# Delta rule's triangular inverse: U made by transposing T, last level on 64x64 blocks

## The chip, the cores and the metric

One core of one Trainium2 chip runs the whole program. The metric is the device time of one execution in microseconds (us), the median of the runs. The engines are PE (TensorE's matmuls), PEld (its weight loads), DVE (VectorE), ACT (ScalarE), POOL (GpSimd) and SP (SyncE, which issues DMAs). Each engine runs its own program in order; semaphores tie them together.

## The reference

A two-layer decoder trunk: layer 0 has an RG-LRU mixer and a dense SwiGLU, layer 1 a gated delta rule (DeltaNet) and a mixture of experts; both have cross-attention. 512 prompt tokens and 8 samples of 4 tokens share the weights. What matters here is the delta rule of layer 1, for 8 heads:

```python
decay = exp(where(lower_incl, gc[..., :, None] - gc[..., None, :], -inf))
A = where(strict_lower, einsum('nbhid,nbhjd->nbhij', kb, k) * decay, 0.0)
Tinv = triangular_solve(A + eye, eye, left_side=True, lower=True, unit_diagonal=True)
u = Tinv @ vb
w = Tinv @ (kb * exp(gc)[..., None])
```

The reference takes chunks of 64 tokens; the kernel takes four chunks of 128 for the prompt, which is the same function, and one small block of 32 for the samples.

## The kernel before

**The inverse.** For each head and each of the four chunks, the inverse of the unit lower triangular 128x128 matrix is built in doubling levels. Level 0 inverts blocks of 2 rows by a subtraction; levels v = 1 to 6 join two blocks of 2^v rows into one of twice the size. The kernel keeps the inverse so far twice: `G_t` (T) and its transpose `G_u` (U), since a matmul wants its left operand transposed. `G_dt` holds the decayed Gram matrix, `G_masks` for each level the blocks that are to be joined. A level goes like this (four chunks at once; `ps` is PSUM, its second index the bank):

- PE, L984: the Gram matrix times T into bank 4. The samples' block, only at level 1, L986.
- DVE, L2131: bank 4 times the level's mask into `G_pt`.
- PE, L1001, not at level 6: U's product with `G_pt` into bank 5; DVE, L2137: T = T - bank 5.
- PE, L1005: the same product the other way round into bank 6; DVE, L2144: U = U - bank 6. At level 1 the samples' U too (L1007, L2143).

After level 6, `G_u` gives the weights and values of the recurrence (L1015, L1025 and on).

**What runs between.** The inverse is a chain, so other work is laid into it by hand, as the order of each engine's program. On PE, `fill(n)` runs n portions of six matmuls (L554) of the input projection of the head after next, two portions after most products, and in places the norms' sums (`lengths`), the transposes of the next head's keys and values (`turn_kv`, L908, L909) and its Gram products (`gram`). Heads 6 and 7 have no head after next, hence no projection left. On DVE, the work on the next two heads follows L2144 of a level: level 1 `argument` (L2004), level 3 `unit` and two taps of `convolve` (L1904, L1909), level 4 `scaled`, `damped` and `out_norm`, level 5 two more taps; `history` comes at level 2 ahead of L2137. POOL splits the arriving weights into two parts (L472, L476) as PE frees their buffers.

**Semaphores.** `d_pt`: bank 4 is full; `d_pte`: `G_pt` is written; `d_ut`: bank 5 is full; `d_tt`: T is written; `d_uu`: bank 6 is full; `d_ute`: U is written. PE waits for `d_tt` ahead of L984 and for `d_pte` and `d_ute` ahead of L1001. `s(...)` on DVE issues an operation and waits until it is done.

Of the kernel before, what the change touches and what calls it, by code (L numbers as in the profile page):

```python
# [5 lines left out]
P = 128  # L6
D, KT = 1024, 8
TP, NB, TS = 512, 8, 4
NS = NB * TS
# [9 lines left out]
GH, C, NC = 8, 128, 4  # L19
NT = NC + 1  # L20
NE, FF, FT = 8, 1536, 12
HALVES = 2
KV1_AT = {0: (0, 4), 1: (4, 8), 2: (8, 12), 3: (12, 16)}
LEVELS = 7
# [87 lines left out]
def ge(eng, sem, val):  # L112

    if isinstance(val, int) and val <= 0:
        return
    eng.wait_ge(sem, val)


def trunk(nc, I, O):
    F, R = mybir.dt.float32, mybir.dt.float32r  # L120
    ALU, ACT, AX = mybir.AluOpType, mybir.ActivationFunctionType, mybir.AxisListType
    MUL, ADD, SUB = ALU.mult, ALU.add, ALU.subtract
    ds = bass.ds

    with ExitStack() as ctx:
# [25 lines left out]
        ps = ctx.enter_context(nc.psum_tensor("ps", [P, 8, 512], F))  # L151
# [388 lines left out]
        def _(pe):  # L540
# [422 lines left out]
            def head(h):  # L963
# [14 lines left out]
                for v in range(1, LEVELS):  # L978
                    small = v < SLEVELS
                    pe.wait_ge(d_tt, h * (LEVELS - 1) + v)  # L980
                    if v == 1:
                        ge(pe, d_s, h * NC)
                    for c in range(NC):
                        last = mm(ps[:, 4, c * P:(c + 1) * P], G_dt[p][:, c, :], G_t[:, c, :], start=True, stop=True)  # L984
                    if small:
                        last = mm(ps[0:NS, 7, 352:352 + NS], G_sdt[0:NS, p, :], G_st[0:NS, :], start=True, stop=True)  # L986
                    last.then_inc(d_pt, 1)
                    fill((2, 2, 2, 2, 3, 3)[v - 1])
                    if v == 1 and h:
                        out_length(h - 1)  # L990
                    if v == 2 and h + 1 < GH:
                        lengths(h + 1, 0)
                    if v == 4 and h + 1 < GH:
                        turn_kv(h + 1)
                    if v == 5 and h + 1 < GH:
                        gram(h + 1)
                    pe.wait_ge(d_pte, h * (LEVELS - 1) + v)
                    pe.wait_ge(d_ute, h * LEVELS + v)
                    if v < LEVELS - 1:
                        for c in range(NC):  # L1000
                            last = mm(ps[:, 5, c * P:(c + 1) * P], G_u[p][:, c, :], G_pt[:, c, :], start=True, stop=True)  # L1001
                        last.then_inc(d_ut, 1)
                    ge(pe, d_vne, h * NC)
                    for c in range(NC):
                        last = mm(ps[:, 6, c * P:(c + 1) * P], G_pt[:, c, :], G_u[p][:, c, :], start=True, stop=True)  # L1005
                    if small:
                        last = mm(ps[0:NS, 7, 384:384 + NS], G_spt[0:NS, :], G_su[0:NS, p, :], start=True, stop=True)  # L1007
                    last.then_inc(d_uu, 1)
                    fill((2, 1, 3, 0, 2, 0)[v - 1])
                    if v == 2 and h + 1 < GH:  # L1010
                        lengths(h + 1, 1)
# [731 lines left out]
        def _(dve):  # L1743
# [373 lines left out]
            def head(h):  # L2117
# [8 lines left out]
                for v in range(1, LEVELS):  # L2126
                    small = v < SLEVELS
                    dve.wait_ge(d_pt, h * LEVELS + v + 1)
                    if small:
                        s(V.tensor_tensor(G_spt[0:NS, :], ps[0:NS, 7, 352:352 + NS], G_masks[0:NS, v - 1, 0:NS], MUL))  # L2130
                    s(V.tensor_tensor(G_pt, b4(4), G_masks[:, v - 1, :].unsqueeze(1).to_broadcast((P, NC, P)), MUL),  # L2131
                      d_pte, h * (LEVELS - 1) + v)
                    if v == 2 and pro:
                        history(h + 2)
                    if v < LEVELS - 1:
# [5 lines left out]
                    dve.wait_ge(d_uu, h * (LEVELS - 1) + v)  # L2141
                    if small:
                        s(V.tensor_tensor(G_su[0:NS, p, :], G_su[0:NS, p, :], ps[0:NS, 7, 384:384 + NS], SUB))  # L2143
                    s(V.tensor_tensor(G_u[p], G_u[p], b4(6), SUB), d_ute, h * LEVELS + (v + 1))  # L2144
                    if v == 1:
                        dve.wait_ge(d_egr, h + 1)
                        s(V.tensor_tensor(G_qg, G_eg[:, p, :], G_qkv[p][:, 0, :], MUL), d_qg, h + 1)
# [292 lines left out]
```

## Time and profile before

| | |
|---|---|
| median of 3 runs | 2546.24 us |
| lowest and highest run | 2544.56 and 2550.89 us |
| span of the profiled execution (its own time, first to last instruction) | 2548.9 us |
| mean granted TensorE clock, share of full speed | 0.958 |
| the eight heads of the delta rule | about 1026 to 1512 us of the span |
| PE busy over the span | 2310.6 us (91%) |
| DVE busy over the span | 905.0 us (36%) |

The profiled execution has no time of its own beside its span; the time around the span is not listed. Busy shares are means over stages with different limits. In a timeline row the first number is the start in us from the span's start, the second the length; `x8` means eight instructions in a row; the bracket is the idle time before and what ended it. A product of four chunks in fp32 shows as eight instructions.

### The profile page before, as it was taken

The page shows a single profiled execution, that of the slowest core. Times are in us where ns is not written, and L with a number is a line of the kernel's source. Part 1 is how long each engine was busy: PE and PEld are TensorE (multiplying, and loading weights), DVE is VectorE, ACT ScalarE, POOL GpSimd, SP SyncE. Part 2 cuts the span into 40 slices and gives each one's busy share as a digit, 9 for nine tenths or more (in the row PEclk, how much of TensorE's full clock was granted, in tenths as well). Part 3 has the DMA queues.
Part 4 walks back from the last instruction along what each step waited for, and adds up shares of the span by engine and source line. Part 5 has one row for each costly group of instructions (what it writes and reads, how often), then busy time and mean ns, then how long its engine had stood idle before and what let it go on. Part 6 is the DMA issues. An engine that isn't in the chain of part 4 may idle for free.

```text
span 2548.9 us, 42792 instructions
## 1 busy us (share of the span) xinstructions
PE 2310.6 (91%) x17174; PEld 2190.4 (86%) x17174; DVE 905.0 (36%) x1485; ACT 541.8 (21%) x1022; POOL 988.9 (39%) x1397
## 2 busy tenths in 40 slices
PE   8998889899999997999999788878599999999993
PEld 8988867899999987888888678848599999999993
DVE  3674423411011158777777545224101000000004
ACT  2351321310011033333333221232100000111103
POOL 4647535588888947333333007705200000000001
PEclk9999999899999999999999889999699999999996
DMA  7314442222222222122122112440456577788884
GB/s 290 99 59 160 157 158 91 91 84 89 92 83 86 87 91 69 52 62 62 62 62 62 37 44 98 182 182 17 178 182 204 193 249 242 241 257 281 280 288 159
DMA packets 98649, 348.08 MB, mean 137 GB/s; under 512 B 13504, under 2 KB 18752, under 8 KB 93616
## 3 DMA queue, kind: packets, MB, share of 16 engines
q1 hardware_dynamic: 73136, 279.08, 32.6%
q10 hardware_dynamic: 19328, 45.18, 5.2%
q0 software_dynamic: 6016, 21.43, 2.3%
q8 instruction: 122, 2.00, 0.3%
q14 instruction: 47, 0.39, 0.1%
HBM read 319.19 MB, written 26.47 MB: 136 GB/s over the span
## 4 chain that ended last, share of the span: by engine, by line
PE 63%; issue 14%; DVE 9%; POOL 6%; DMA 4%; ACT 3%; ACTq 0%; POOLq 0%; DVEq 0%; SPq 0%
PE ps L554 26%; PE ps L1144 14%; PE ps L1159 8%; PE ps L794 4%; POOL wl L476 3%; DMA raw<-weights 3%; POOL wh L472 2%; PE ps L655 1%; DVE x L1770 1%; PE ps L1005 1%; PE ps L1001 1%; PE ps L984 1%; PE ps L659 1%; PE ps L841 1%; DVE x L1758 1%
## 5 line engine op out<-in xcount | busy, mean ns | idle before, releaser
L472 POOL TENSOR_TENSOR wh<-raw,tab 128x256 fp32r<-128x256 f32 x672 | 439.7, 685 | 806.3 <-PE ps L554 541.2
L476 POOL TENSOR_TENSOR wl<-raw,wh 128x256 fp32r<-128x256 f32 x672 | 521.1, 806 | 0.0
L1144 PE MATMUL ps<-work,raw 128*128 128x128 f32 (+6 forms) x3072 | 424.3, 299 | 13.0 <-DMA raw<-weights 10.6
L1144 PEld LDWEIGHTS ps<-work,raw 128*128 128x128 f32 x3072 | 419.6, 191 | 16.3 <-issue 9.4
L554 PE MATMUL ps<-xh,wh 128*128 128x272 f32 x2048 | 306.1, 300 | 49.0 <-POOL wl L476 17.0
L554 PEld LDWEIGHTS ps<-xh,wh 128*128 128x128 f32 x2048 | 276.7, 195 | 63.6 <-issue 26.1
L554 PE MATMUL ps<-xh,wl 128*128 128x272 f32 x2048 | 297.5, 295 | 0.0
L554 PE MATMUL ps<-xl,wh 128*128 128x272 f32 x2048 | 280.9, 289 | 0.0
L554 PEld LDWEIGHTS ps<-xh,wl 128*128 128x128 f32 x2048 | 275.8, 194 | 1.8 <-issue 0.5
L554 PEld LDWEIGHTS ps<-xl,wh 128*128 128x128 f32 x2048 | 266.1, 189 | 0.0
L523 POOL DMA_DIRECT2D rows_y<-moe_h x8 | 4.3, 540 | 656.9 <-DVE moe_h L2255 656.9
L1159 PE MATMUL ps<-work,raw 128*128 128x128 f32 (+6 forms) x1536 | 218.0, 298 | 1.6 <-DVE work L2262 0.8
L1159 PEld LDWEIGHTS ps<-work,raw 128*128 128x128 f32 x1536 | 209.6, 190 | 2.4 <-DVE work L2262 1.4
L2262 DVE TENSOR_TENSOR work<-moe_h,ps 128x128 f32<-128x128 f32 (+6 forms) x96 | 30.6, 319 | 438.4 <-ACT moe_h L1678 438.4
L1678 ACT ACTIVATE moe_h<-ps 128x128 f32<-128x128 f32 (+6 forms) x96 | 29.1, 303 | 396.7 <-PE ps L1144 396.7
L1854 DVE TENSOR_TENSOR work<-work,ps 128x544 f32<-128x544 f32 x24 | 17.3, 721 | 228.6 <-PE ps L554 228.6
L2255 DVE COPY moe_h<-ps 128x256 f32<-128x256 f32 (+1 forms) x64 | 25.0, 391 | 198.0 <-PE ps L1132 155.5
L794 PE MATMUL ps<-hh,wh 128*128 128x272 f32 x384 | 79.7, 289 | 0.9 <-POOL wl L476 0.9
L794 PE MATMUL ps<-hh,wl 128*128 128x272 f32 x384 | 79.0, 288 | 0.0
L794 PE MATMUL ps<-hl,wh 128*128 128x272 f32 x384 | 78.9, 287 | 0.0
L1246 ACT ACTIVATE lnr<-x 128x544 f32<-128x544 f32 x35 | 23.1, 660 | 216.0 <-DVE x L1806 159.0
L1806 DVE SCALAR_TENSOR_TENSOR x<-x,ps 128x544 f32<-128x544 f32 x32 | 23.1, 721 | 124.3 <-PE ps L554 119.1
(378 smaller groups left out, 2987.3 us busy)
## 6 DMA issues: line engine op xcount, KB each, us to landing
raw<-weights SPq DMA_DIRECT2D x488, 512.0 KB, 4.1
moe_h<-cache SPq DMA_DIRECT2D x6, 2048.0 KB, 9.2
moe_h<-cache ACTq DMA_DIRECT2D x4, 2048.0 KB, 15.3
work<-cache SPq DMA_DIRECT2D x4, 2048.0 KB, 8.7
moe_h<-rows_x POOLq DMA_DIRECT2D x14, 512.0 KB, 8.0
rows_x<-lnsq ACTq DMA_DIRECT2D x9, 512.0 KB, 10.9
work<-scratch ACTq DMA_DIRECT2D x16, 272.0 KB, 4.2
work<-cache ACTq DMA_DIRECT2D x2, 2048.0 KB, 10.5
```

The source lines that it names most:

```text
L472: nc.gpsimd.tensor_tensor(flat(h1[:, k0:k1]), flat(r1[:, k0:k1]), one_col, MUL).then_inc(pool_hi, 1)
L476: low = nc.gpsimd.tensor_tensor(flat(l1[:, k0:k1]), flat(r1[:, k0:k1]), flat(h1[:, k0:k1]).bitcast(F), SUB)
L554: last = mm(ps[:, 2 * i + h, 0:HT], w[:, par_, k, :], a[:, k, h * HT:(h + 1) * HT], start=(n == 0 and k == 0), stop=(n == 2 and k == KT - 1))
L655: last = mm(ps[:, b, 0:MEM], raw[:, q, k, :], A_mem[:, k, :], start=(k == 0), stop=(k == KT - 1))
L659: last = mm(ps[:, b, mt * P:(mt + 1) * P], A_mem[:, k, mt * P:(mt + 1) * P], raw[:, q, k, :], start=(k == 0), stop=(k == KT - 1))
L794: last = mm(ps[:, 2 * d + h, 0:HT], w[:, s % 2, k, :], a[:, f, h * HT:(h + 1) * HT], start=(f == 0 and m == 0), stop=(f == FT - 1 and m == 2))
L841: last = mm(ps[:, 4 + 2 * (g % 2) + h, 0:HT], L_gw[:, 4 * k + g, :], L_rec[:, b % 2, k, h * HT:(h + 1) * HT], start=(k == 0), stop=(k == 1))
L984: last = mm(ps[:, 4, c * P:(c + 1) * P], G_dt[p][:, c, :], G_t[:, c, :], start=True, stop=True)
L1144: last = mm(ps[:, j // 2, (j % 2) * c:(j % 2 + 1) * c], raw[:, slot % RAW, k, :], M_x[:, r % 2, k, 0:c], start=(k == 0), stop=(k == KT - 1))
L1159: last = mm(ps[:, 2 + d % 2, 0:c], raw[:, slot % RAW, k, :], M_h[:, f, 0:c], start=(f == 0), stop=(f == FT - 1))
L1678: s(A(M_s[:, f % 2, 0:c], ps[:, f % 2, 0:c], ACT.Silu), m_silu, e12 + f + 1)
L2262: s(V.tensor_tensor(M_h[:, f, 0:c], M_s[:, f % 2, 0:c], ps[:, f % 2, c:2 * c], MUL), m_h, e12 + f + 1)
```

## The change

At levels 1 to 5, U is no longer computed by a product and a subtraction. When the new T is there, PE transposes it into bank 6 at the start of the next level, ahead of that level's product into bank 4, and DVE copies bank 6 into U. The samples' block at level 1 stays as it was, without a signal of its own. At level 6 only the lower left quarter of the product is computed (64x64x64), the mask becomes a copy of that quarter, the last product is 64x64x64 as well, and U's upper right quarter is written as its negative. The wait for bank 6 (`d_vne`) moves to the first transposes.

```diff
--- before.py
+++ after.py
@@ -19,6 +19,7 @@
 GH, C, NC = 8, 128, 4
 NT = NC + 1
 NE, FF, FT = 8, 1536, 12
+HP = P // 2
 HALVES = 2
 KV1_AT = {0: (0, 4), 1: (4, 8), 2: (8, 12), 3: (12, 16)}
 LEVELS = 7
@@ -980,8 +981,17 @@
                     pe.wait_ge(d_tt, h * (LEVELS - 1) + v)
                     if v == 1:
                         ge(pe, d_s, h * NC)
+                    else:
+                        if v == 2:
+                            ge(pe, d_vne, h * NC)
+                        for c in range(NC):
+                            last = nc.tensor.transpose(ps[:, 6, c * P:(c + 1) * P], G_t[:, c, :], ident)
+                        last.then_inc(d_uu, 1)
                     for c in range(NC):
-                        last = mm(ps[:, 4, c * P:(c + 1) * P], G_dt[p][:, c, :], G_t[:, c, :], start=True, stop=True)
+                        if v < LEVELS - 1:
+                            last = mm(ps[:, 4, c * P:(c + 1) * P], G_dt[p][:, c, :], G_t[:, c, :], start=True, stop=True)
+                        else:
+                            last = mm(ps[HP:P, 4, c * P:c * P + HP], G_dt[p][0:HP, c, HP:P], G_t[0:HP, c, 0:HP], start=True, stop=True)
                     if small:
                         last = mm(ps[0:NS, 7, 352:352 + NS], G_sdt[0:NS, p, :], G_st[0:NS, :], start=True, stop=True)
                     last.then_inc(d_pt, 1)
@@ -1000,12 +1010,13 @@
                         for c in range(NC):
                             last = mm(ps[:, 5, c * P:(c + 1) * P], G_u[p][:, c, :], G_pt[:, c, :], start=True, stop=True)
                         last.then_inc(d_ut, 1)
-                    ge(pe, d_vne, h * NC)
-                    for c in range(NC):
-                        last = mm(ps[:, 6, c * P:(c + 1) * P], G_pt[:, c, :], G_u[p][:, c, :], start=True, stop=True)
-                    if small:
-                        last = mm(ps[0:NS, 7, 384:384 + NS], G_spt[0:NS, :], G_su[0:NS, p, :], start=True, stop=True)
-                    last.then_inc(d_uu, 1)
+                        if small:
+                            mm(ps[0:NS, 7, 384:384 + NS], G_spt[0:NS, :], G_su[0:NS, p, :], start=True, stop=True)
+                    else:
+                        for c in range(NC):
+                            last = mm(ps[0:HP, 6, c * P + HP:(c + 1) * P], G_pt[HP:P, c, 0:HP], G_u[p][HP:P, c, HP:P],
+                                      start=True, stop=True)
+                        last.then_inc(d_uu, 1)
                     fill((2, 1, 3, 0, 2, 0)[v - 1])
                     if v == 2 and h + 1 < GH:
                         lengths(h + 1, 1)
@@ -2128,8 +2139,11 @@
                     dve.wait_ge(d_pt, h * LEVELS + v + 1)
                     if small:
                         s(V.tensor_tensor(G_spt[0:NS, :], ps[0:NS, 7, 352:352 + NS], G_masks[0:NS, v - 1, 0:NS], MUL))
-                    s(V.tensor_tensor(G_pt, b4(4), G_masks[:, v - 1, :].unsqueeze(1).to_broadcast((P, NC, P)), MUL),
-                      d_pte, h * (LEVELS - 1) + v)
+                    if v < LEVELS - 1:
+                        s(V.tensor_tensor(G_pt, b4(4), G_masks[:, v - 1, :].unsqueeze(1).to_broadcast((P, NC, P)), MUL),
+                          d_pte, h * (LEVELS - 1) + v)
+                    else:
+                        s(V.tensor_copy(G_pt[HP:P, :, 0:HP], b4(4)[HP:P, :, 0:HP]), d_pte, h * (LEVELS - 1) + v)
                     if v == 2 and pro:
                         history(h + 2)
                     if v < LEVELS - 1:
@@ -2141,7 +2155,11 @@
                     dve.wait_ge(d_uu, h * (LEVELS - 1) + v)
                     if small:
                         s(V.tensor_tensor(G_su[0:NS, p, :], G_su[0:NS, p, :], ps[0:NS, 7, 384:384 + NS], SUB))
-                    s(V.tensor_tensor(G_u[p], G_u[p], b4(6), SUB), d_ute, h * LEVELS + (v + 1))
+                    if v < LEVELS - 1:
+                        s(V.tensor_copy(G_u[p], b4(6)), d_ute, h * LEVELS + (v + 1))
+                    else:
+                        s(V.tensor_scalar(G_u[p][0:HP, :, HP:P], b4(6)[0:HP, :, HP:P], -1.0, None, MUL),
+                          d_ute, h * LEVELS + (v + 1))
                     if v == 1:
                         dve.wait_ge(d_egr, h + 1)
                         s(V.tensor_tensor(G_qg, G_eg[:, p, :], G_qkv[p][:, 0, :], MUL), d_qg, h + 1)
```

## Rows read from the trace of the kernel before

**Rows 1.** Windows, heads 4 and 6: us, then busy us (instructions) of PE, PEld, DVE, ACT, POOL; PEclk; DMA.

```profile
1281.30:1344.60 63.30, 59.68 (x483) 55.35 (x483) 46.30 (x82) 21.14 (x42) 21.95 (x33) 1.00 0.21 62
...
1407.90:1466.10 58.20, 44.17 (x289) 37.48 (x289) 33.13 (x60) 15.46 (x29) 4.58 (x6) 0.85 0.09 30
```

**Rows 2.** Groups by line, DVE, the eight heads: busy, mean ns, idle before, releasers.

```profile
L2131 DVE TENSOR_TENSOR work<-ps,moe_h 128x512 f32<-128x512 f32 x48 | 33.2, 691 | 16.8 <-PE ps L984 15.3 <-DVE work L2005 0.2
...
L2137 DVE TENSOR_TENSOR moe_h<-moe_h,ps 128x512 f32<-128x512 f32 x40 | 27.5, 688 | 60.0 <-PE ps L1001 59.7
```

**Rows 3.** Timeline of head 4, levels 1 to 3: start, length, engine, line.

```profile
1288.31 0.69 DVE L2144 TENSOR_TENSOR work<-work,ps 128x512 f32<-128x512 f32 x1
...
1289.41 0.98 PEld L984 LDWEIGHTS ps<-moe_h,work 128*128 128x128 f32 x8
...
1291.62 0.69 DVE L2131 TENSOR_TENSOR work<-ps,moe_h 128x512 f32<-128x512 f32 x1
...
1292.61 1.09 PEld L1001 LDWEIGHTS ps<-work 128*128 128x128 f32 x8
...
1294.00 0.69 DVE L2137 TENSOR_TENSOR moe_h<-moe_h,ps 128x512 f32<-128x512 f32 x1
...
1296.07 1.09 PEld L984 LDWEIGHTS ps<-moe_h,work 128*128 128x128 f32 x8
...
1298.58 0.99 PEld L1001 LDWEIGHTS ps<-work 128*128 128x128 f32 x8
```

**Rows 4.** Timeline of head 4, levels 3 to 5.

```profile
1300.76 0.69 DVE L2144 TENSOR_TENSOR work<-work,ps 128x512 f32<-128x512 f32 x1 [0.20 <-PE ps L1005]
...
1302.63 0.98 PEld L984 LDWEIGHTS ps<-moe_h,work 128*128 128x128 f32 x8
...
1304.40 0.69 DVE L2131 TENSOR_TENSOR work<-ps,moe_h 128x512 f32<-128x512 f32 x1
...
1306.13 0.97 PEld L1001 LDWEIGHTS ps<-work 128*128 128x128 f32 x8
...
1308.30 0.69 DVE L2144 TENSOR_TENSOR work<-work,ps 128x512 f32<-128x512 f32 x1 [0.20 <-PE ps L1005]
...
1314.84 0.69 DVE L2131 TENSOR_TENSOR work<-ps,moe_h 128x512 f32<-128x512 f32 x1
...
1315.58 0.97 PEld L1001 LDWEIGHTS ps<-work 128*128 128x128 f32 x8 [0.75 <-DVE work L2131]
```

**Rows 5.** Timeline of head 4, levels 5 and 6.

```profile
1317.74 0.69 DVE L2144 TENSOR_TENSOR work<-work,ps 128x512 f32<-128x512 f32 x1 [0.20 <-PE ps L1005]
...
1318.86 0.98 PEld L984 LDWEIGHTS ps<-moe_h,work 128*128 128x128 f32 x8
...
1320.64 0.69 DVE L2131 TENSOR_TENSOR work<-ps,moe_h 128x512 f32<-128x512 f32 x1
...
1322.00 0.98 PEld L1005 LDWEIGHTS ps<-work 128*128 128x128 f32 x8
...
1323.28 0.69 DVE L2144 TENSOR_TENSOR work<-work,ps 128x512 f32<-128x512 f32 x1 [1.07 <-PE ps L1005]
```

**Rows 6.** Timeline: transposes of the next head's keys.

```profile
1305.04 0.48 PEld L908 LDWEIGHTS ps<-tab,x 128*128 128x128 f32 x4
...
1305.48 0.10 PEld L909 LDWEIGHTS ps<-tab,x 128*32 128x32 f32 x1
```

**Rows 7.** Single DVE lines, whole kernel: ns min/median/max, first and last start.

```profile
L2174 DVE COPY work<-ps x8: 292/293/293, 1077.0 to 1503.2; 128x128 f32<-128x128 f32 x8
...
L2004 DVE SCALAR_TENSOR_TENSOR work<-work,tab x32: 351/352/695, 999.0 to 1419.2; 128x128 f32<-128x128 f32 x32
...
L1909 DVE SCALAR_TENSOR_TENSOR work<-work,par x64: 810/812/1172, 55.6 to 1405.0; 128x568 f32<-128x568 f32 x64
```

**Rows 8.** Timeline, POOL: first part of the weight splitting.

```profile
1292.17 2.33 POOL L472 TENSOR_TENSOR wh<-raw,tab 128x256 fp32r<-128x256 f32 x4 [6.21 <-PE ps L554]
...
1305.40 2.33 POOL L472 TENSOR_TENSOR wh<-raw,tab 128x256 fp32r<-128x256 f32 x4 [8.15 <-PE ps L554]
```

## What the change does to the time: the prediction

> **What bounds the kernel now.** I read the page first (span 2548.9 us; TensorE busy nearly throughout), then the stretch of the delta rule alone, because all edits lie in its eight heads. The windows table gives one line a head. Head 4 takes 63.3 us, with PE busy 59.7 and DVE 46.3 at a granted clock of 1.00; head 6, which has no projection work left to fill with, takes 58.2 us at 0.85 [rows 1]. Heads 0 to 5 repeat head 4's pattern (head 0 is a little shorter). A busy share of 94% looks as if PE set the time. The groups by line and the timeline say something else: the two engines hand data to and fro inside each level, each in its own program order. Over the eight heads DVE waited 59.7 us before the subtraction from T (L2137) for the product L1001, and 15.3 us before the mask (L2131) for L984 [rows 2]. So I follow one head through its levels and ask at each hand-over which side comes last.
>
> Names, for level v: P is the product into bank 4 (L984), M the mask (L2131), Q the product into bank 5 (L1001), S the subtraction giving the new T (L2137), R the old product into bank 6 (L1005), U the update of U (L2144), F the projection matmuls that PE runs between them. In head 4 DVE runs S and U back to back and then its other work for the next heads (history, argument, unit, convolve, scaled, damped, out_norm), while PE runs R, then F, then the next P. At levels 2, 3 and 4 Q starts straight after PE's own preceding work: P3 to Q3 takes 2.51 us [rows 3]. At level 5 it starts 0.74 us after M, that is as M ends [rows 4]. Both sides are nearly balanced, and DVE's side work is hidden under F.
>
> **The change, part by part.** *R at levels 1 to 5 goes.* Eight matmul instructions per R (an fp32 product shows as two). Q3 to P4 is 4.05 us for Q, R and eighteen F matmuls [rows 3, 4]; of an eight-instruction product PE's issue is 0.88 us (eight at 0.11, the spacing below). *Four transposes come in its place*, after the wait for the new T and ahead of the next P. The transposes of the key rows, of the same kind and 128x128 size, show as one instruction each: four start 0.44 us before the next group, so 0.11 us each [rows 6]. PE therefore issues 0.44 us less per level. A result reaches DVE 1.28 us after an eight-instruction product starts (L1005 at 1322.00, U at 1323.28 [rows 5]); with four fewer, 1.28 - 0.44 = 0.84 us after the first transpose.
>
> But the place matters more than the work. Before, U's operand was computed before F; now DVE's copy into U waits until PE has run F, has seen the new T and has transposed it. Behind that copy on DVE stand all the side jobs of the level, then M; PE's next Q waits for M. U's copy itself costs what the subtraction did (a copy lies on the same line of sizes, below), so nothing is gained there.
>
> Head 4, with a dash for the time after the change. I move P back by the 0.88 us of the missing R wherever PE's own work sets it.
> - Level 1 to 2: P2 was at 1289.41, so the transposes start at 1288.53; U', behind the sample rows' small subtraction (0.21 with its gap), at 1288.53 + 0.84 + 0.21 = 1289.58, 1.27 later than 1288.31. M2' follows at 1291.62 + 1.27 = 1292.89, Q2' 0.75 later (M's 0.69 and 0.06) at 1293.64 instead of 1292.61: **+1.03** [rows 3]. PE, ready at 1288.97 + 3.20 = 1292.17, waits about 1.5 us.
> - Level 2 to 3: transposes at Q2' + (3.46 - 0.88) = 1296.22 (S, at 1294.00 + 1.27 and 0.69 long, is done), P3' 1296.66, Q3' 2.51 later, 1299.17: +0.59 in all, so **0.44 given back** [rows 3].
> - Level 3 to 4: transposes at 1299.17 + 4.05 - 0.88 = 1302.34, U' at 1303.18, 2.42 later than 1300.76. Two normalisations and two convolution taps follow; M4' 3.64 after U' at 1306.82, Q4' 1307.57 against 1306.13: **+1.44 in all** [rows 4].
> - Level 4 to 5: no F here, so S ends last: 1.28 + 0.69 + 0.05 = 2.02 after Q4', then 0.84: U' at 1310.43 against 1308.30. M5' 6.54 later, Q5' at 1317.71 against 1315.58: **+2.13 in all** [rows 4].
> - Level 5 to 6: transposes at Q5' + (3.28 - 0.88) = 1320.11, U' 1320.95, M6' 2.90 later at 1323.85 [rows 5].
> - *Level 6, 64x64.* M becomes a copy of 4x64 columns. A 128-column copy takes 0.29 [rows 7], a 512-column operation 0.69 [rows 2]; a straight line gives 0.42 for 256. The last R starts at 1323.85 + 0.42 + 0.06 = 1324.33. No 64-column product is in the trace: at 128 columns' price DVE goes on 1.28 later, at half the issue 0.84; I take 0.84, since the 0.11 spacing is that of 128 moving columns. U's last step, again 256 columns, 0.42: done at 1325.59. Before: 1323.28 + 0.69 = 1323.97 [rows 5]. **Head 4: +1.6 us**; with both 64x64 savings nil, 0.27 + 0.44 + 0.27 more, +2.6. The smaller P of level 6 saves nothing: F and U's side work cover it.
>
> *A collision.* POOL's splitting starts when F ends a weight tile: 1292.17 and 1305.40, some 2.76 us after P2 and P4 [rows 8]. P moves earlier than, or with, its old place and DVE's side work moves later, so the last of the four 128x128 operations of the argument and the convolution tap now run under POOL. Those operations take 352 ns alone and up to 695, the tap 812 and up to 1172 [rows 7]. Nil to 0.69 (two of the four) and nil to 0.36: I take one of each, 0.34 + 0.36 = **0.7 a head**.
>
> Heads 0 to 5: 6 x (1.6 + 0.7) = 13.8 us. Heads 6 and 7 have no F: each of five levels puts 0.44 between S and P, up to 2.2; where M follows P at once, this is on the path (that wait is the 15.3 us of [rows 2]). Level 6 gives back 0.98. That is +1.2 at most; nil if the lengths and side work still end later. I take 0.7 each. Sum: 13.8 + 1.4 = **+15 us**. Nothing after the heads has slack against them: the output projection reads their result. The profiled span, 2548.9, is 2.7 above the runs' median; added to the median, 2546.2 + 15 = 2561.
>
> The Trainium skill's "TensorEngine Tiling (Array Packing)", sections Overview and Tiling Modes, says that a 64x64 product uses one of four independent tiles, at best four times the rate. No row here shows 64x64; all four chunks use the same tile in this diff, so I don't count on it. By that rule the last R's issue would be an estimated 0.22 instead of 0.44, the sum 8 x 0.22 = 1.8 us less.
>
> **The rivals.**
> 1. *PE's own work is the bound after all* (faster). Place: heads 0 to 5, PE busy 94%. If no M ends after F, only PE's savings count: 5 x 0.44 + 0.44 = 2.6 us a head, 8 heads, 21 us: 2525. For it: Q2 to Q4 start behind PE's own work. Against: those have less than a microsecond of slack, while U moves 1.3 to 3.2 us. It decides only if DVE's copy into U can come within about 0.3 us of the old place. Chance 0.07.
> 2. *The delays are swallowed* (same): F that no longer fits moves to the head's end, where PE waits often, and the 64x64 steps are cheaper than taken. Six heads at nil to 1 us: 2546 to 2553. Chance 0.13.
> 3. *The clock falls.* With more idle time and fewer matmuls, heads 0 to 5 could behave as head 6, granted 0.85 [rows 1]. A mean of 0.85 is 0.30 of the stretch at 1.2 GHz, at most 0.15 x 63 = 9.5 us of PE time a head; with a quarter on the path, 2.4 x 6 = 14 us more: 2575. Against: head 4 already has waits of 0.5 to 1 us without a fall. The Trainium skill's "Perfetto Trace Analysis", Matmul Optimizations, speaks for this rival: power scales with utilisation, so matmuls should run back to back; head 6's row agrees. Chance 0.10.
> 4. *The forecast*: 2554 to 2573. Lower end: no collision, 6 x 1.6 = 9.6, less up to 2 for cheaper small steps. Upper end: both collisions whole (1.05) and the 64x64 savings nil (2.6): 6 x 3.65 + 4 = 26. Chance 0.70.
>
> **How the numbers follow.** The bound for no change is 0.3%, 7.6 us, so 2538.6 to 2553.9. Faster 0.07 (rival 1), same 0.13 (rival 2), slower 0.80 (forecast and rival 3). The range reaches from the middle of rival 2, 2550, to the low edge of rival 3, 2574; what lies outside is rival 1, half of 2 and part of 3.
>
> **What would show it.** Right: in a head with F, U's copy waits for the transposes, 2 us and more at levels 3 and 5; Q2, Q4 and Q5 wait for M; the heads 0 to 5 become about 2.3 us longer, 6 and 7 by less than 1.5; transposes at 0.11 us spacing; the argument or the tap lengthened under POOL. Wrong: heads shorter than 63.3 us, Q still directly behind F at levels 3 to 5, or PEclk under 1.00 in heads 0 to 5, which would put the cost elsewhere.

## The result and the profile after

The changed kernel takes 2585.04 us (median of 4 runs, 2581.29 to 2590.43) beside 2548.56 us for the kernel before (4 runs on the same chip, 2544.56 to 2551.18): ratio 1.0137, 95% interval 1.0115 to 1.0159. It is slower, as forecast, but by 36 us and not by 15, and the time lies outside the range.

The two profiled spans differ by 30.6 us (2548.9 and 2579.5). Up to head 0's first subtraction (before L2123, now L2134) the profiles differ by -1.5 us; the eight heads, from there to the last copy of outputs, go from 482.0 to 513.5 us, **+31.5**; the rest of the program differs by +0.6. So in these two profiles the whole loss lies in the heads, where the edits are. The profiled execution of the changed kernel is the fastest of its four; the others took longer at lower mean granted clocks (spans of 2579.5, 2581.5, 2584.9 and 2588.6 us at 0.947, 0.945, 0.943 and 0.937), so the medians differ by more than the two profiles.

The windows of the kernel after: heads 3, 4 and 6, then head 7 up to U's last step, and from there to the outputs. Columns as in [rows 1].

```profile
1228.50:1294.20 65.70, 57.84 (x463) 52.11 (x462) 47.01 (x82) 21.09 (x42) 22.70 (x33) 1.00 0.21 60
1294.20:1361.67 67.47, 60.77 (x463) 55.00 (x462) 47.02 (x81) 21.09 (x42) 22.70 (x33) 0.95 0.19 58
...
1427.36:1488.32 60.96, 43.44 (x269) 36.00 (x269) 32.65 (x60) 15.50 (x29) 4.59 (x6) 0.80 0.09 29
1488.32:1520.40 32.08, 20.52 (x124) 17.14 (x124) 17.34 (x27) 5.37 (x6) 0.00 (x0) 0.83 0.10 33
1520.40:1545.00 24.60, 21.09 (x105) 17.64 (x106) 6.76 (x12) 4.49 (x10) 0.00 (x0) 0.50 0.01 3
```

The same stretch from U's last step of head 7, in the kernel before:

```profile
1496.87:1515.00 18.13, 13.82 (x104) 11.15 (x105) 7.05 (x12) 4.50 (x10) 0.00 (x0) 0.88 0.02 5
```

Two kinds of loss are to be seen. Head 3 ran at full clock throughout (1.00, as head 4 before in [rows 1]) with PE doing 1.8 us *less* than there, and still took 65.70 instead of 63.3 us. Heads 1 and 5 agree (65.76, 65.69). Head 4 did the same instructions in 67.47 us at a granted clock of 0.95, and everything after U's last step in head 7 ran at 0.50, which is 1.2 of 2.4 GHz. A stretch granted 0.50 is called a half-rate stretch below.

DVE's groups in the eight heads show what the copy into U waits for. U's old subtraction (L2144) had waited 15.2 us for PE in all.

```profile
L2159 DVE COPY work<-ps 128x512 f32<-128x512 f32 x40 | 27.7, 692 | 41.7 <-PE ps L988 41.3 <-DVE work L2157 0.2
L2143 DVE TENSOR_TENSOR work<-ps,moe_h 128x512 f32<-128x512 f32 x40 | 27.7, 692 | 3.4 <-PE ps L992 2.3
L2151 DVE TENSOR_TENSOR moe_h<-moe_h,ps 128x512 f32<-128x512 f32 x40 | 27.5, 688 | 54.7 <-PE ps L1011 54.5
...
L2015 DVE SCALAR_TENSOR_TENSOR work<-work,tab 128x128 f32<-128x128 f32 x28 | 13.1, 466 | 1.0
```

The waits of [rows 2] have changed places: the mask, which had waited 15.3 us for PE, now waits 2.3, for it is late itself. DVE stands 41.3 us before a copy whose data comes from the four transposes (L988). The timeline of head 3 shows where (L2159 U's copy, L2143 and L2146 M, L1011 Q, L994 and L1017 the 64x64 products):

```profile
1235.70 0.48 PEld L988 LDWEIGHTS ps<-tab,moe_h 128*128 128x128 f32 x4
...
1236.73 0.69 DVE L2159 COPY work<-ps 128x512 f32<-128x512 f32 x1
...
1238.22 2.06 DVE L2015 SCALAR_TENSOR_TENSOR work<-work,tab 128x128 f32<-128x128 f32 x4
...
1238.90 2.42 POOL L473 TENSOR_TENSOR wh<-raw,tab 128x256 fp32r<-128x256 f32 x4 [5.76 <-PE ps L555]
...
1240.83 0.69 DVE L2143 TENSOR_TENSOR work<-ps,moe_h 128x512 f32<-128x512 f32 x1
...
1241.57 0.97 PEld L1011 LDWEIGHTS ps<-work 128*128 128x128 f32 x8 [2.27 <-DVE work L2143]
...
1242.46 0.80 PEld L555 LDWEIGHTS ps<-xh,wh 128*128 128x128 f32 x6
...
1250.97 0.69 DVE L2159 COPY work<-ps 128x512 f32<-128x512 f32 x1 [2.01 <-PE ps L988]
...
1253.77 1.04 DVE L1920 SCALAR_TENSOR_TENSOR work<-work,par 128x568 f32<-128x568 f32 x1
...
1255.58 0.97 PEld L1011 LDWEIGHTS ps<-work 128*128 128x128 f32 x8 [1.31 <-DVE work L2143]
...
1265.65 0.97 PEld L1011 LDWEIGHTS ps<-work 128*128 128x128 f32 x8 [0.76 <-DVE work L2143]
...
1268.68 0.54 PEld L994 LDWEIGHTS ps<-moe_h,work 64*64 64x64 f32 x8 [0.17 <-issue]
...
1271.77 0.43 DVE L2146 COPY work<-ps 64x256 f32<-64x256 f32 x1
...
1272.25 0.54 PEld L1017 LDWEIGHTS ps<-work 64*64 64x64 f32 x8 [0.66 <-DVE work L2146]
...
1273.14 0.42 DVE L2161 TENSOR_SCALAR work<-ps 64x256 f32<-64x256 f32 x1
```

At level 2 the order is plain: transposes, copy, argument (2.06 us for four, partly under POOL's splitting), mask, and only then Q, for which PE has stood 2.27 us. At level 4 PE waits 1.31 us, at level 5 0.76.

Head 2 shows the second loss. The windows of its first half, and two timeline rows that answer to those of head 3 at 1241.57 and 1242.46:

```profile
1161.06:1174.10 13.04, 11.24 (x83) 10.08 (x81) 9.59 (x16) 5.35 (x12) 7.27 (x11) 1.00 0.18 52
1174.10:1179.00 4.90, 4.86 (x24) 4.29 (x25) 2.49 (x4) 0.33 (x1) 2.53 (x4) 0.65 0.23 80
1179.00:1190.00 11.00, 9.96 (x83) 9.47 (x82) 6.46 (x9) 7.42 (x12) 2.51 (x4) 1.00 0.09 36
1190.00:1196.00 6.00, 5.15 (x31) 4.96 (x31) 3.86 (x7) 0.00 (x0) 3.30 (x5) 0.72 0.35 118
```

```profile
1174.14 0.97 PEld L1011 LDWEIGHTS ps<-work 128*128 128x128 f32 x8 [2.27 <-DVE work L2143]
...
1175.02 1.42 PEld L555 LDWEIGHTS ps<-xh,wh 128*128 128x128 f32 x6
```

Behind the same wait of 2.27 us the granted clock is 0.65 over 4.9 us, and six projection matmuls take 1.42 us to issue instead of 0.80. This makes Q of level 3 start 1.6 us later than in head 3, counted from the head's first subtraction. A second such stretch, 0.72 over 6.0 us, follows the waits of level 4 (1.31 us ahead of Q, then 1.04 ahead of the transposes) and adds only 0.15 us to the head. In this profile heads 0, 2 and 4 have a granted clock below 1.00, heads 1, 3 and 5 do not, though PE's waits are as long in head 3.

### The profile page after: what moved, and what is told of

The parts are those of the page before. It is cut to its first block, busy times and chain, and to the rows that moved or that the text cites. A ratio compares the mean times of both kernels' runs of the same rounds, so it can differ in the third digit from the quotient of the medians.

```text
span 2579.5 us, 42479 instructions
## 1 busy us (share of the span) xinstructions
PE 2308.6 (89%) x17014; PEld 2179.6 (84%) x17014; DVE 908.5 (35%) x1485; ACT 541.4 (21%) x1022; POOL 994.2 (39%) x1397
## 4 chain that ended last, share of the span: by engine, by line
PE 61%; issue 15%; DVE 12%; POOL 6%; DMA 4%; ACT 2%; ACTq 0%; DVEq 0%; POOLq 0%; SPq 0%
PE ps L555 24%; PE ps L1155 14%; PE ps L1170 8%; PE ps L795 4%; POOL wl L477 3%; DMA raw<-weights 3%; POOL wh L473 2%; PE ps L656 1%; DVE x L1781 1%; PE ps L1011 1%; DVE work L1920 1%; PE ps L660 1%; PE ps L842 1%; DVE x L1769 1%; DVE work L2159 1%
## 5 line engine op out<-in xcount | busy, mean ns | idle before, releaser
L473 POOL TENSOR_TENSOR wh<-raw,tab 128x256 fp32r<-128x256 f32 x672 | 444.9, 692 | 829.4 <-PE ps L555 554.5
L2280 DVE TENSOR_TENSOR work<-moe_h,ps 128x128 f32<-128x128 f32 (+6 forms) x96 | 30.6, 319 | 442.3 <-ACT moe_h L1689 442.3
L1011 PE MATMUL ps<-work 128*128 128x128 f32 x320 | 47.6, 295 | 29.2 <-DVE work L2143 29.2
L1011 PEld LDWEIGHTS ps<-work 128*128 128x128 f32 x320 | 41.8, 202 | 36.6 <-DVE work L2143 35.4
## 6 DMA issues: line engine op xcount, KB each, us to landing
moe_h<-cache ACTq DMA_DIRECT2D x4, 2048.0 KB, 14.6
```

The costliest lines, as they stand in the source:

```text
L473: nc.gpsimd.tensor_tensor(flat(h1[:, k0:k1]), flat(r1[:, k0:k1]), one_col, MUL).then_inc(pool_hi, 1)
L2280: s(V.tensor_tensor(M_h[:, f, 0:c], M_s[:, f % 2, 0:c], ps[:, f % 2, c:2 * c], MUL), m_h, e12 + f + 1)
```

## The experiments

All kernels were compared with the kernel before on the same chip. The profiled heads are given as periods, from one first subtraction to the next.

**1. The copy behind the side work.** PE is left as changed. On DVE the copy into U and its wait move behind the level's side work, to just ahead of the next mask.

```diff
+                    if v > 1:
+                        dve.wait_ge(d_uu, h * (LEVELS - 1) + v - 1)
+                        if v == 2:
+                            s(V.tensor_tensor(G_su[0:NS, p, :], G_su[0:NS, p, :], ps[0:NS, 7, 384:384 + NS], SUB))
+                        s(V.tensor_copy(G_u[p], b4(6)), d_ute, h * LEVELS + v)
                     dve.wait_ge(d_pt, h * LEVELS + v + 1)
...
-                    dve.wait_ge(d_uu, h * (LEVELS - 1) + v)
...
-                        s(V.tensor_copy(G_u[p], b4(6)), d_ute, h * LEVELS + (v + 1))
```

> The changed kernel with one thing moved: on DVE the copy into U (and its wait for the transposes) comes after the level's side work, just ahead of the next mask, in place of ahead of the side work. PE's program is untouched. Theory of the place (U's late copy holds up DVE's side work and with it the next mask): heads 0 to 5 fall from 65.7 us (67.4 with the slower clock) to about 61, below the 63.3 of before, since PE's issue is shorter by 0.44 a level; heads 6 and 7 stay about 1 us above before; the time about 2536 us, 12 under before. Rival, the clock (PE is granted less because it does less, wherever DVE's copy stands): half-rate stretches still appear in heads 0 to 5 and just after head 7, and the time stays above 2560. Rival, PE's own work: no difference from the changed kernel.

Measured: 2534.84 us, ratio 0.9945 (0.9926 to 0.9963). It takes 50 us less than the changed kernel and is faster than the kernel before. Head 2 in the windows, DVE's groups, and level 2 in the timeline (copy L2143, mask L2148):

```profile
1146.77:1207.40 60.63, 56.73 (x463) 52.20 (x462) 46.18 (x81) 21.09 (x42) 21.86 (x33) 1.00 0.20 65
```

```profile
L2148 DVE TENSOR_TENSOR work<-ps,moe_h 128x512 f32<-128x512 f32 x40 | 27.7, 691 | 5.4 <-PE ps L992 4.4
L2143 DVE COPY work<-ps 128x512 f32<-128x512 f32 x40 | 27.7, 691 | 14.1 <-PE ps L988 13.1
...
L2015 DVE SCALAR_TENSOR_TENSOR work<-work,tab 128x128 f32<-128x128 f32 x28 | 9.9, 352 | 1.0
```

```profile
1153.97 1.51 DVE L2015 SCALAR_TENSOR_TENSOR work<-work,tab 128x128 f32<-128x128 f32 x4
...
1156.00 0.69 DVE L2143 COPY work<-ps 128x512 f32<-128x512 f32 x1
...
1156.73 0.69 DVE L2148 TENSOR_TENSOR work<-ps,moe_h 128x512 f32<-128x512 f32 x1
...
1157.62 1.09 PEld L1011 LDWEIGHTS ps<-work 128*128 128x128 f32 x8
```

The copy's wait falls from 41.3 to 13.1 us, the argument is back at 352 ns an operation because it runs ahead of POOL's splitting, Q of levels 2 to 4 no longer waits (at level 5 it still waits 1.23 us for the mask), and the head takes 60.63 us with no half-rate stretch. Of heads 0 to 5 only head 3 had one (61.39 us at 0.97); head 7, which has no projection work, took 50.70 us at 0.70, where it had taken 46.39 before. PE's program is the changed kernel's, so the copy's *place* in DVE's order was the cost; the transposes themselves are a gain (run 2).

**2. Level 6 alone.** The kernel before, with only level 6 on 64x64 blocks: P, mask, R and U's last step, all as in the change's diff.

```diff
                     for c in range(NC):
-                        last = mm(ps[:, 6, c * P:(c + 1) * P], G_pt[:, c, :], G_u[p][:, c, :], start=True, stop=True)
+                        if v < LEVELS - 1:
+                            last = mm(ps[:, 6, c * P:(c + 1) * P], G_pt[:, c, :], G_u[p][:, c, :], start=True, stop=True)
+                        else:
+                            last = mm(ps[0:HP, 6, c * P + HP:(c + 1) * P], G_pt[HP:P, c, 0:HP], G_u[p][HP:P, c, HP:P],
...
```

> The kernel before with level 6 alone changed (products 64x64x64, copy of the quarter for the mask, U's quarter written as the negative); levels 1 to 5 keep the product and the subtraction for U. Theory of the place: level 6 gives back about 1 us a head (0.27 on the mask, 0.3 to 0.4 on the product, 0.27 on U), 8 us in all, so about 2540 us; all of the loss lies with the transposes. Rival: the 64x64 products cost as much as the 128 ones, and the time is that of before within 3 us. Rival, the clock: less work on PE lowers the clock, and the time is above before.

Measured: 2546.39 us, ratio 0.9993 (0.9979 to 1.0006): the same. A head takes 62.63 instead of 63.28 us, so 0.65 and not 1.0 is gained (5 us over eight heads, which is the lower end of that interval); the small R begins only as F ends, so the smaller mask is hidden. Beside run 1's 60.63 us, the transposes with their copy behind the side work are worth 2.0 us a head.

**3. The old product at the transposes' place.** The changed kernel, with U's product and subtraction where transposes and copy stand.

```diff
-                            last = nc.tensor.transpose(ps[:, 6, c * P:(c + 1) * P], G_t[:, c, :], ident)
+                            last = mm(ps[:, 6, c * P:(c + 1) * P], G_pt[:, c, :], G_u[p][:, c, :], start=True, stop=True)
...
-                        s(V.tensor_copy(G_u[p], b4(6)), d_ute, h * LEVELS + (v + 1))
+                        s(V.tensor_tensor(G_u[p], G_u[p], b4(6), SUB), d_ute, h * LEVELS + (v + 1))
```

> The changed kernel with the old product and the old subtraction for U put at the very place of the transposes and of the copy (start of the next level, ahead of its first product); level 6 as changed. It has as many products as before at levels 1 to 5, and PE is as busy. Theory of the place: as slow as the changed kernel and about 0.44 us a level more where U's copy is on the path, so 67 to 68 us a head with projection work, 8 to 16 us above the changed kernel, about 2595 us. Rival, the clock: with the work back on PE no half-rate stretch appears in heads 0 to 5, and it is faster than the changed kernel by 5 us or more.

Measured: 2597.75 us, ratio 1.0193 (1.0171 to 1.0215), heads at 68.03 us. With the same operation as before the change at levels 1 to 5, only at its late place, the kernel loses 49 us; transposing instead gives 2.3 us a head back (68.03 to 65.70). Three of heads 0 to 5 had a half-rate stretch (granted 0.97 to 0.98), though PE has no transposes here and as many products at these levels as before.

**4. Idle products, first try.** The changed kernel with four extra products of `G_dt` and the identity ahead of the mask's wait at levels 1, 3 and 5, and after Q at level 4 and in heads 6 and 7. Here and below these products only keep PE at work; their bank is overwritten unread.

```diff
+                    if h + 2 < GH and v in (1, 3, 5):
+                        pe.wait_ge(d_ute, h * LEVELS + v)
+                        idle(4)
...
+                    if v < LEVELS - 1 and (v == 4 or h + 2 >= GH):
+                        idle(4)
```

> The changed kernel with four idle 128x128 products (0.88 us) laid into PE's waits: ahead of the mask's wait at levels 1 and 3 and ahead of the Gram products at level 5 in heads 0 to 5, after the product into bank 5 at level 4 and in heads 6 and 7 at levels 1 to 5. Their results are overwritten unread. Theory of the place alone: nothing gained, each head as in the changed kernel or up to 0.5 us longer, time 2585 or a little above. The clock as second term: the half-rate stretches in heads 0, 2 and 4 and after head 7 go, heads 0 to 5 all at about 65.7 us, and the time falls by 8 to 14 us to about 2573.

Measured: 2593.04 us, ratio 1.0174 (1.0152 to 1.0196): a miss. PE has no wait at levels 1 and 3 (it waits at 2, 4 and 5), so twice 0.9 us of idle products were put on the path: the heads at full clock took 67.45 to 67.50 us, 1.8 more. Half-rate stretches still came, in four of heads 0 to 5.

**5. Idle products in the real waits.** Seven at level 2, four at levels 4 and 5 ahead of Q; four after Q at level 4 and in head 7.

```diff
+                    if h + 1 < GH and v in (2, 4, 5):
+                        pe.wait_ge(d_ute, h * LEVELS + v)
+                        idle(7 if v == 2 else 4)
```

> The changed kernel with idle 128x128 products in the waits that its trace shows: seven (1.5 us) ahead of the mask's wait at level 2 (2.3 us there), four (0.9 us) at level 4 and ahead of the Gram products at level 5, for heads 0 to 6; four after the product into bank 5 at level 4, and in head 7 at all levels. The idle products of the earlier attempt stood at levels 1 and 3, where PE has no wait. The clock as second term (a long wait of PE is followed by a half-rate stretch that slows the next products): heads 0 to 5 all at 65.7 us, no half-rate stretch in them, the time 6 to 12 us under the changed kernel. Rival (the stretches come whatever PE does): heads 2 and 4 or others still at 67.4 us, the time as the changed kernel or a little above.

Measured: 2572.25 us, ratio 1.0096 (1.0079 to 1.0114), 8.6 us less than the unmodified changed kernel on the same chip (run 8); the single times of the two do not overlap. Where the gain lies is less clear: in the two profiles only 2.1 us of it are in the eight heads (509.6 and 507.5 us), and 7.6 us are ahead of head 0, where both run the same code. In head 2's windows the clock no longer falls behind the waits of levels 2 and 4; one fall came later, as the inverse ended and the recurrence began. PE's row shows the fill, 14 weight loads, ahead of a Q that now waits 0.47 us:

```profile
1157.86:1176.00 18.14, 17.86 (x136) 16.57 (x135) 13.46 (x22) 7.44 (x15) 9.80 (x14) 1.00 0.21 60
1176.00:1200.00 24.00, 23.10 (x189) 21.73 (x189) 15.02 (x24) 6.30 (x11) 5.81 (x8) 1.00 0.19 71
1200.00:1210.00 10.00, 8.61 (x79) 7.21 (x78) 7.38 (x17) 3.75 (x9) 5.52 (x8) 0.83 0.15 54
...
1512.00:1533.70 21.70, 19.84 (x102) 16.62 (x102) 4.02 (x8) 3.37 (x9) 0.00 (x0) 0.50 0.01 4
```

```profile
1235.64 1.76 PEld L975 LDWEIGHTS ps<-tab,work 128*128 128x128 f32 x14
1237.87 0.97 PEld L1018 LDWEIGHTS ps<-work 128*128 128x128 f32 x8 [0.47 <-DVE work L2152]
```

In heads at full clock the fills cost nothing (65.69 us). The last window, after head 7's inverse, still ran at 0.50.

**6. The transposes alone.** The changed kernel with level 6 as it was before.

```diff
-                    if v < LEVELS - 1:
-                        s(V.tensor_tensor(G_pt, b4(4), G_masks[:, v - 1, :].unsqueeze(1).to_broadcast((P, NC, P)), MUL),
-                          d_pte, h * (LEVELS - 1) + v)
-                    else:
-                        s(V.tensor_copy(G_pt[HP:P, :, 0:HP], b4(4)[HP:P, :, 0:HP]), d_pte, h * (LEVELS - 1) + v)
+                    s(V.tensor_tensor(G_pt, b4(4), G_masks[:, v - 1, :].unsqueeze(1).to_broadcast((P, NC, P)), MUL),
+                      d_pte, h * (LEVELS - 1) + v)
...
```

> The changed kernel with level 6 as before (128x128x128 products, the mask over 512 columns, the subtraction for U); levels 1 to 5 with transposes. Theory of the place: the transposes carry all of the loss and level 6 gives back 0.98 us a head in the changed kernel, where the last mask ends last (0.27 + 0.44 + 0.27), so heads 0 to 5 about 66.7 us and the time about 8 us above the changed kernel, 2593. Rival: level 6 is nothing, and the time is that of the changed kernel within 3 us.

Measured: 2580.69 us, ratio 1.0129 (1.0108 to 1.0149). The heads are longer by 0.9 us (66.63), as expected, yet the time is that of the changed kernel and not 8 us above it. Heads 1 to 5 all ran at 1.00, behind the same waits of PE as in the changed kernel; head 3, and its Q of level 2:

```profile
1229.88:1296.51 66.63, 58.44 (x463) 52.87 (x462) 47.61 (x81) 21.09 (x42) 22.25 (x33) 1.00 0.20 59
```

```profile
1242.95 0.97 PEld L1008 LDWEIGHTS ps<-work 128*128 128x128 f32 x8 [2.26 <-DVE work L2138]
```

Head 7 took 56.3 us instead (50.5 in run 8). So level 6's gain shows in the heads at full clock; in the whole time it is lost among half-rate stretches that come in one execution and not in another.

**7. P ahead of the transposes.** Run 1's kernel, with heads 0 to 5 issuing P first and then the transposes.

```diff
-                        for c in range(NC):
-                            last = nc.tensor.transpose(ps[:, 6, c * P:(c + 1) * P], G_t[:, c, :], ident)
-                        last.then_inc(d_uu, 1)
+                        if h + 2 >= GH:
+                            turn()
...
                     last.then_inc(d_pt, 1)
+                    if v > 1 and h + 2 < GH:
+                        turn()
```

> The version with U's copy behind the side work, and in heads 0 to 5 the product into bank 4 ahead of the transposes (heads 6 and 7 keep the transposes first). Theory of the place: at level 5, where the new T ends last, the product starts 0.44 us earlier and the transposes fall into the projection work; elsewhere nothing. So 0.4 us a head, heads 0 to 5 at about 60.2 in place of 60.6, and the time 2 to 3 us under the version before it, about 2533. Rival: the transposes' results come too late for the copy, which now waits ahead of the mask, and nothing is gained.

Measured: 2536.46 us, ratio 0.9950 (0.9930 to 0.9969), the same as run 1; heads 60.92 instead of 60.63 us, so the rival was right. At level 3 the mask, whose data comes sooner, stands behind a copy whose data comes later:

```profile
1227.24 0.69 DVE L2149 COPY work<-ps 128x512 f32<-128x512 f32 x1 [2.31 <-PE ps L975]
...
1227.96 0.69 DVE L2154 TENSOR_TENSOR work<-ps,moe_h 128x512 f32<-128x512 f32 x1
```

**8. The changed kernel again,** unmodified, beside runs 5 to 7.

> The changed kernel once more, with a second profile. If the half-rate stretches belong to it, heads of 65.7 us and of about 67.4 us alternate again and a long half-rate stretch follows head 7, with the time again 2581 to 2590. If they were that one execution's, the heads in the second profile are all 65.7 us and the span is about 2565.

Measured: 2580.85 us, ratio 1.0131 (1.0115 to 1.0147). The falls come back at the same two places of a head: in head 2, 0.65 over 4.9 us behind level 2's wait, and 0.69 over 5.5 us behind level 4's. Which heads get them differs: head 3 at 65.70 us has no fall again, head 0 took 63.26 (66.12), and heads 1 and 5 now take 68.64 and 67.32. From U's last step in head 7 to the outputs this profile took 16.9 us, where the first had taken 22.1 at 0.50, with no edit between them. The two falls of head 2, and that end:

```profile
1178.80:1183.70 4.90, 4.86 (x24) 4.30 (x25) 2.48 (x4) 0.31 (x1) 2.53 (x4) 0.65 0.24 79
...
1195.00:1200.50 5.50, 4.65 (x27) 4.46 (x26) 3.59 (x7) 0.00 (x0) 3.01 (x5) 0.69 0.30 97
...
1526.43:1543.30 16.87, 14.48 (x102) 11.70 (x102) 4.39 (x8) 2.90 (x9) 0.00 (x0) 0.76 0.00 1
```

**9. Run 1's kernel with the waits of heads 6 and 7 filled.** These heads have no projection; `late` is true in them. The idle products write bank 0, so at the start of both heads PE also waits until the last projection has been read out of it (`d_z`). Nine more follow head 7's last product.

```diff
+                late = h + 2 >= GH
+                if late:
+                    pe.wait_ge(d_z, GH)
...
+                    if late and v > 1:
+                        spare(3)
                     pe.wait_ge(d_pte, h * (LEVELS - 1) + v)
...
+                if late:
+                    spare(4)
                 pe.wait_ge(d_wte, h + 1)
...
+                    if late and c in (1, 2):
+                        spare(2)
```

> The kernel with U's copy behind the side work, and in addition idle products where PE waits in heads 6 and 7, which have no projection: three ahead of each mask wait from level 2, four after Q where the next T is waited for, four ahead of the wait for the weights of the recurrence, two at two of its chunks, nine after the last product of head 7's inverse. They write a bank whose content is overwritten unread. Before them heads 6 and 7 had granted clocks of 0.79, 0.67 and 0.74 and took 56.05 and 50.70 us to the last output copy. Theory (half rate follows PE's waits, and the rest of the loss after head 7 is that): the granted clock stays near 1.00 in both heads, head 6 takes about 54, head 7 about 45; the time is about 2527, 8 us below the kernel without them. Rival (the late stretch has another cause, or the idle products delay the chain by what the clock gives): a half-rate stretch still follows head 7's inverse, or the heads stay at 56 and 50; 2533 to 2540.

Measured: 2531.32 us, ratio 0.9931 (0.9914 to 0.9948). Head 6 takes 53.66 us (56.05 without), head 7 45.64 (50.70). The windows of head 7:

```profile
1445.71:1455.70 9.99, 8.76 (x36) 7.68 (x37) 5.57 (x8) 4.68 (x5) 0.00 (x0) 0.52 0.08 31
1455.70:1491.50 35.80, 33.43 (x289) 29.68 (x288) 16.29 (x28) 3.72 (x10) 0.00 (x0) 1.00 0.07 22
```

Its beginning, up to level 1's products, still ran at 0.52; from level 2 on the clock is 1.00 to the outputs, where in run 1 a stretch of 20 us (1466.75 to 1486.75) ran at 0.50. Beside run 1's profile the two heads take 7.5 us less, as the theory said. But run 7, whose program for heads 6 and 7 is run 1's, took as little in head 7 without any fill:

```profile
1451.07:1496.48 45.41, 32.72 (x226) 26.91 (x226) 21.73 (x36) 8.29 (x15) 0.00 (x0) 0.85 0.07 24
```

So only head 6's gain holds against both profiles (56.30 us in run 7), and that the fills shorten head 7 is not shown. The time is 4 us above the theory: the two profiles differ by 5.3 us in the rest of the program after the heads (1040.9 and 1035.6), where they run the same code. The intervals of runs 1 and 9 overlap; that 9 is the faster kernel is likely and not shown.

**10. Run 5's kernel with the end filled as well.**

```diff
+                if late:
+                    spare(4)
...
+                    if late and c in (1, 2):
+                        spare(2)
...
+            for c in range(9):
+                mm(ps[:, 0, c % NC * P:(c % NC + 1) * P], G_dt[1][:, c % NC, :], ident, start=True, stop=True)
             out_length(GH - 1)
```

> The changed kernel with the real waits filled, as before (2572 us, where head 7's last stretch still ran at a granted clock of 0.50, 21.7 us long), and in addition idle products in heads 6 and 7 ahead of the wait for the weights of the recurrence (four), at two of its chunks (two each) and after head 7's inverse (nine). Theory: the stretch from U's last step in head 7 to the last output copy runs at 1.00 and takes about 15 instead of 21.7 us; the time is about 2566. Rival: the granted clock falls there whatever PE does in these waits; the stretch stays at 20 us or more and the time at 2572.

Measured: 2567.17 us, ratio 1.0069 (1.0051 to 1.0086). From U's last step in head 7 to the outputs:

```profile
1521.00:1537.20 16.20, 15.80 (x129) 13.78 (x130) 4.16 (x8) 3.13 (x9) 0.00 (x0) 0.89 0.01 2
```

These are 16.2 us at 0.89 instead of run 5's 21.7 at 0.50, near the theory's number. But run 8 had taken 16.9 us at 0.76 there without any fill, so this is no more than two profiles of one kernel differ by. And in this profile a stretch of 17 us at 0.50 came in head 6 (61.85 us, in run 5 57.25). Against run 8 the gain of all fills together is clear (ratio 1.0069 beside 1.0131, intervals apart); against run 5 it is not (the intervals overlap).

## Why the prediction missed

**Right: which hand-over goes bad, and by how much.** In a head at full clock the forecast was +2.3 us, with the collision; measured is 65.70 less 63.28, **+2.4**. The steps, each as delay against the head before (head 3 after against head 4 before; forecast with the argument's collision in it, which falls between U' and M' of level 2, and the tap's at level 4):

| start of | forecast | measured |
|---|---|---|
| U' after level 1 | +1.27 | +1.23 |
| M' level 2 | +1.61 | +2.02 |
| Q' level 2 | +1.37 | +1.77 |
| Q' level 3 | +0.93 | +1.21 |
| U' after level 3 | +2.76 | +3.02 |
| Q' level 4 | +2.14 | +2.26 |
| U' after level 4 | +2.83 | +2.87 |
| U' after level 5 | +3.91 | +3.93 |

The rows fit "Behind that copy on DVE stand all the side jobs of the level, then M; PE's next Q waits for M". The level-by-level sum follows one chain through both engines, and it held within 0.4 us. The last row agrees better than the ones above it: a surplus of 0.40 us at Q' of level 2 shrinks to 0.02 by U' after level 5, so the closeness of the end is in part luck.

**Collision: right in kind, 1.0 a head instead of 0.7.** The argument's four took 2.06 instead of 1.5 us, its small one 0.48 instead of 0.24 (together +0.79 where 0.34 was taken), the tap 1.04 instead of 0.81 (+0.23 for 0.36). Run 1 confirms it from the other side: the argument ahead of POOL's splitting is back at 352 ns.

**Transposes and level 6.** Four transposes issue in 0.48 us (0.44 taken). From the small R's start to U's last step are 0.89 us (0.84 taken); mask and last step are 0.43 and 0.42 us, as the line between 128 and 512 columns gave. "I take 0.84" was thus the right end of its bounds. The Trainium skill's "TensorEngine Tiling (Array Packing)" (Overview) gives a 64x64 product as one of four independent tiles; the eight here, all on the same partitions, issue in 0.54 us where eight 128x128 ones take 0.97 in the same trace. All runs put the four chunks on the same partitions, so none tests tiles side by side.

**Right sum, heads 0 to 5.** 6 x 2.43 = 14.6 us for the waits, forecast 13.8. Head 6 takes 2.7 us more, at a granted clock of 0.80 where it was 0.85, and head 7 up to U's last step 1.3 (30.76 to 32.08 us); forecast 0.7 each. In these two heads no experiment tells the waits from the clock: in run 8 they are 0.8 and 2.8.

**The step that failed: the clock, which the forecast's sum puts at nothing.** The terms above make 14.6 + 2.7 + 1.3 = 18.6 of the 31.5 us. The rest is 6.3 us in heads 0, 2 and 4 (2.8, 1.7 and 1.8 above the +2.43 of a head at full clock) and 6.5 us from head 7's last U step to the outputs (15.6 to 22.1 us), where the granted clock stood below 1.00 (0.95 in head 4, 0.50 after head 7). In run 8's profile it is 8.2 us in heads 1, 2, 4 and 5, and 1.3 after head 7's last U step. The prediction had this only as rival 3, "The clock falls": 14 us on top of the forecast (2561 + 14 = 2575), in heads 0 to 5 alone, at a chance of 0.10. It held against it that "head 4 already has waits of 0.5 to 1 us without a fall". That was no evidence on the new waits: its own step for level 1 to 2 had PE waiting "about 1.5 us" (2.27 came), longer than any wait it had cited. Its sign of being wrong, "PEclk under 1.00 in heads 0 to 5", came in three heads of six. With the rival's 14 in the sum, 15 + 14 = 29 of the 31.5 us would have come out, but partly by luck: those 14 were for heads 0 to 5, which lost 6.3 and 8.2 us in the two profiles, and nothing was set down for the end of head 7.

**What the falls hang on.** PE's new waits are the likely cause; the runs do not show it in full. Half-rate stretches that begin in heads 0 to 5, one number for each profile:

| U's operand | profiles | stretches |
|---|---|---|
| not late, or copied behind the side work | before, runs 2, 1, 7, 9 | 0, 0, 1, 0, 0 |
| late, level 2's wait not filled | changed kernel, runs 8, 3, 4, 6 | 6, 7, 3, 4, 1 |
| late, waits of levels 2, 4 and 5 filled | runs 5, 10 | 3, 0 |

So they come with the late copy. Neither the transposes nor the smaller number of products explains them: runs 1 and 7 have both, and one stretch between them; run 3 has neither at levels 1 to 5, and three stretches. With products in the real waits none begins behind the filled waits of levels 2 and 4, and the kernel takes 8.6 us less (run 5). "Perfetto Trace Analysis" (Matmul Optimizations) in the Trainium skill says that matmuls should run back to back; those 8.6 us agree. Against a rule as simple as "a wait brings a fall" stands run 6, whose heads 1 to 5 have the same waits and no fall.

**Rival 1** ("PE's own work is the bound after all", 2525) was wrong for this change, and right for the kernel with one edit more. Its condition was "only if DVE's copy into U can come within about 0.3 us of the old place"; run 1 meets its sense in another way, by letting the mask follow directly on the copy with the side work ahead of both. Its 2.65 us a head (63.28 to 60.63) is near the 2.6 that this rival had, in part by luck: Q of levels 2, 3 and 4 gain 0.44, 0.47 and 0.47 us, as the rival had it, Q of level 5 only 0.17, and the other 1.1 come behind it.

**Open.** Which heads get a half-rate stretch: two profiles of one kernel gave heads 0, 2, 4 and heads 1, 2, 4, 5 behind equal waits. Open too is why run 6's heads 1 to 5 had none behind the same waits, and why the end of head 7 took 22.1 us in one profile of the changed kernel and 16.9 in the other. And a fall that is filled away in one place sometimes comes at another (head 2's recurrence in run 5, head 6 in run 10).

## What to carry to other kernels

When an operation is moved to a later point of another engine, its consumer should move too: an in-order engine that waits for late data holds everything queued behind it, and the same 463 PE instructions gave +36 us or -14 us by the place of one copy. Where two engines hand data to and fro, follow the chain level by level with durations from the timeline; that held here within 0.4 us. New waits of PE need a clock term in the forecast's own sum, on top of the waiting, with a wide range. And before a shorter stretch is put down to an edit, a second profile of the unedited kernel should be read: here the same code differed by 5 us in the end of head 7.

## What the hardware showed that was not expected

A wait of 2.27 us in a stretch that otherwise runs at 1.00 can be followed by 4.9 us at a granted 0.65, which costs 1.6 us: six 128x128 loads go from 0.80 to 1.42 us. It need not be: in run 6 five heads with this wait stayed at 1.00. Products without any use, in those waits, shortened the kernel by 8.6 us (run 5 beside run 8), though its heads by only 2.1 in the two profiles. Eight 64x64 loads issue in 0.54 us where eight of 128x128 take 0.97, but they start behind an issue gap of 0.17 us, so of the 0.43 us saved 0.26 is left.
